# A hybrid attention and convolution layer on eight cores: casts ahead of the row factors, deferred VectorE work let out by a cost count, and the last output tile finished bank by bank

## What is computed

```python
h = rms_norm(x, norm_pre_w, NORM_EPS)
q, k, v, z_a, u_glu, z_c, ga, gc = split(h @ w_in)        # widths 1024 x4, 2048, 1024, 2048, 2048
q, k = partial_rotary(q), partial_rotary(k)               # 8 heads, two softmax maps of 64 each
o = diff_attention(q, k, v, lam)                          # softmax(q1 k1) v - lam softmax(q2 k2) v, causal
y_attn = (rms_norm(o, subln_w, SUBLN_EPS) * (1 - lam_init) * silu(z_a)) @ w_o_attn
u = causal_depthwise_conv(glu(u_glu + b_glu), w_dw, b_dw) # width 31
u = silu(layer_norm(u)) * silu(z_c)
y_conv = u @ w_pw2 + b_pw2
m = sigmoid(ga) * y_attn + sigmoid(gc) * y_conv
out = x + rms_norm(m @ w_out, norm_post_w, NORM_EPS)
```

## Time and profile before

| | us |
|---|---|
| median of 3 runs (lowest, highest) | 1183.71 (1183.11, 1189.87) |
| the profiled execution | 1181.25 |
| its span, slowest core | 1179.7 |
| TensorE busy | 1096.0 (93%) |
| VectorE busy | 551.1 (47%) |
| ScalarE busy | 323.7 (27%) |

### The profile page before, as it was taken

The page is one execution under the profiler, slowest core; times in us unless marked ns, Lnnn a source line. Parts: engine busy times, 40 slices in busy tenths (PEclk is TensorE's granted clock), DMA queues, the critical chain, the costliest instruction groups (busy, mean ns, idle before and its releaser), DMA issues.

```text
span 1179.7 us, 21808 instructions; the slowest of 8 cores (1168.9 to 1179.7 us)
## 1 busy us (share of the span) xinstructions
PE 1096.0 (93%) x8042; PEld 674.0 (57%) x8042; DVE 551.1 (47%) x1290; ACT 323.7 (27%) x500; POOL 102.1 (9%) x196
## 2 busy tenths in 40 slices
PE   2699999999999998899888999999999999999995
PEld 1355556886666774577444566666666666654442
DVE  5573444426556136766677633333333333315333
ACT  3442223432101165566444311111111111102111
POOL 1111010011101100000000001101101010000000
PEclk9899999999999998899899999999999999999998
DMA  8929767554665632322142305337266183064442
GB/s 251 220 46 174 143 114 150 106 86 81 139 135 113 139 57 57 57 49 51 37 73 37 55 18 108 55 53 114 46 128 110 34 144 57 16 179 161 158 160 95
DMA packets 49792, 118.11 MB, mean 100 GB/s; under 512 B 5520, under 2 KB 11920, under 8 KB 46352
## 3 DMA queue, kind: packets, MB, share of 16 engines
q0 software_dynamic: 27648, 62.93, 32.8%
q1 hardware_dynamic: 21744, 53.53, 14.9%
q10 hardware_dynamic: 288, 0.18, 0.0%
HBM read 162.94 MB, written 16.58 MB: 152 GB/s over the span
## 4 chain that ended last, share of the span: by engine, by line
PE 81%; DVE 9%; issue 3%; DMA 3%; ACT 3%; DVEq 0%; SPq 0%; ACTq 0%
PE ps L1291 21%; PE ps L816 11%; PE ps L1343 11%; PE ps L770 10%; PE ps L649 9%; PE ps L1301 5%; PE ps L1295 5%; PE ps L693 3%; PE ps L1021 2%; PE ps L922 2%; DMA r<-usc 2%; PE ps L899 2%; DVE zoz L970 1%; DVE r L1028 1%; DVE r L958 1%
## 5 line engine op out<-in xcount | busy, mean ns | idle before, releaser
L1291 PE MATMUL ps<-hTo,wring 128*128 128x384 bf16 x1536 | 257.5, 326 | 0.0
L1291 PEld LDWEIGHTS ps<-hTo,wring 128*128 128x128 bf16 x1536 | 150.3, 98 | 99.2
L164 POOL DMA_DIRECT2D wring<-wp x176 | 93.4, 549 | 835.9 <-PE ps L1291 242.0
L649 PE MATMUL ps<-hTo,wring 128*128 128x384 bf16 x768 | 130.9, 332 | 9.9 <-ACT hTo L545 4.2
L770 PE MATMUL ps<-wring,hTo 128*128 128x256 bf16 x1152 | 135.6, 273 | 1.2 <-PE ps L899 1.2
L1308 ACT ACTIVATE zoz<-zoz 128x384 f32<-128x384 f32 x96 | 50.0, 522 | 315.3 <-DVE zoz L1306 315.3
L816 PE MATMUL ps<-hTo,wring 128*128 128x384 bf16 x768 | 125.0, 326 | 0.0
L770 PEld LDWEIGHTS ps<-wring,hTo 128*128 128x128 bf16 x1152 | 108.6, 98 | 21.2 <-issue 8.3
L1306 DVE TENSOR_TENSOR zoz<-ps,R 128x384 f32<-128x384 f32 x96 | 53.5, 558 | 128.0 <-PE ps L1291 127.8
L649 PEld LDWEIGHTS ps<-hTo,wring 128*128 128x128 bf16 x768 | 75.6, 100 | 63.1 <-issue 16.5
L905 ACT ACTIVATE r<-ps 128x1024 bf16<-128x1024 f32 (+2 forms) x104 | 92.8, 905 | 47.6 <-PE ps L899 44.2
(11 more groups left out here) (114 smaller groups left out, 1016.1 us busy)
## 6 DMA issues: line engine op xcount, KB each, us to landing
wring<-wp POOLq DMA_DIRECT2D x176, 256.0 KB, 7.1
r<-usc SPq DMA_DIRECT2D x32, 295.2 KB, 8.2
hTo<-xr SPq DMA_DIRECT2D x9, 1024.0 KB, 6.8
out<-hTo SPq DMA_DIRECT2D x18, 512.0 KB, 3.3
r<-xf SPq DMA_DIRECT2D x11, 768.0 KB, 9.2
r<-wop POOLq DMA_DIRECT2D x4, 1024.0 KB, 13.8
zoz<-wop POOLq DMA_DIRECT2D x4, 1024.0 KB, 14.9
r<-wout POOLq DMA_DIRECT2D x4, 1024.0 KB, 20.5
```

Of the source, the lines that this page charges most:

```text
L164: eng.dma_start(out=it[1][0], in_=it[1][1]).then_inc(self.dsem[it[2]], 16)
L649: t.op('pe', lambda e, dc=dc, x=x: e.matmul(bank(2 * par + x, n), lhsT=w[:, dc, 128 * x:128 * x + 128], rhs=hTo[:, dc, c:c + n], start=(dc ...
L1291: t.op('pe', lambda e, dc=dc, k=k, w=w, o=o, cs=cs, c0=c0, n=n: e.matmul(o[k], lhsT=w[:, dc, cs], rhs=hTo[:, dc, HALO + c0:HALO + c0 + n], ...
```

## The change

1. **Start.** On the program's TensorE queue the first GLU stands ahead of the first column sums, quarter by quarter (`quart`). `own_run` is taken apart: the casts of the next group stand ahead of the roots and factors of the one before, squares and sums behind. `own_sums` loses its root and diagonals to a new `own_roots`. GLU pairs use banks 0/1, 2/3 or 4/5 by hand. The weight panel 3 waits for the last x quarter.
2. **Attention.** `run_late(H.rate)` gives way to `pump()`: two running sums, `now['pe']` and `now['dve']`, are raised by `spent` with costs written in the source; a deferred operation leaves the list only when `now['pe']` has reached its `ready` mark and `now['dve']` is at most 0.5 above it. `finalize` still forces what is older than four slots. The tanh and the two products of a z_conv evacuation go on a second list, `zlate`, from which one entry is taken at each step. The pieces are dealt out otherwise (`H.fill`): on the first half z_conv channel blocks 0 and 1 in the first pair of heads, 2 and 3 in the second, 4 in the third, 5 to 7 in the last, where it was 0, 1, 2 and 3 to 7.
3. **Merge.** The gates and y_conv of two blocks (`merge_head` 0 and 1) stand ahead of the last two heads' transposes.
4. **Last tile.** `g_last` squares each bank as it is finished and multiplies it; after the last bank come a reduction of four sums, the root, and four multiply-adds of 512 columns with a store each, by turns from the SP and ScalarE queues.

```diff
+            self.fill = ((('v', 1), ('z', 0, 1)), (('v', 2), ('z', 2, 3)), (('v', 3), ('z', 4)), (('z', 5, 6, 7),))
...
+        step = 4 if quart else 16
+        for k, (d0, x) in enumerate((d0, x) for d0 in range(0, 16, step) for x in (1, 0)):
+            for dc in range(d0, d0 + step):
...
+    def spent(e, us):
+
+        now[e] = (max(now['dve'], now['pe']) if e == 'dve' else now['pe']) + us
...
+        spent('pe', w / 1280.0)
...
+                spent('dve', 0.3)
...
+        spent('pe', 0.16 * len(todo))
...
+    def pump():
+
+        while late and late[0][1] <= now['pe'] and now['dve'] <= now['pe'] + 0.5:
+            run_late(1)
+
+    def run_zlate(flush=False):
+
+        while zlate:
+            zlate.pop(0)()
+            if not flush:
+                return
...
-        late.extend((fk, x) for x in f)
+        ready = now['pe'] + (2.0 if half == 0 else 0.0)
+        late.extend((fk, ready, 0.4, x) for x in f)
...
-            late.extend((fk + 1, x) for x in f)
+            late.extend((fk + 1, ready, 0.3, x) for x in f)
...
-            run_late(H.rate)
+            run_zlate()
+            pump()
...
+                run_zlate(True)
                 t.op('dve', lambda e: e.tensor_tensor(out=zv, in0=bank(b, n), in1=rv, op=ALU.mult), reads=[('ps', b)] + rn, writes=[('zt', p)])
...
+                zlate.extend((tanh, prods))
...
                 fill[done]()
+                spent('pe', 0.8)
+                pump()
...
+    glu_mm(0, 0, 0, quart=True)
     own_sums(0)
...
+    own_half(4)
+    own_half(5)
+    own_roots(0)
+    own_half(6)
+    own_half(7)
+    own_sq(4)
+    own_sq(5)
...
+    glu_mm(0, 1, 2, quart=True)
+    own_factors(0)
+    glu_ev(0, 0)
+    own_sum(4)
...
+    glu_mm(1, 2, 0)
     own_sums(2)
-    glu_mm(1, 2)
+    own_roots(2)
+    glu_mm(2, 2, 2)
     own_factors(2)
...
+                if it == 0:
+                    merge_head(0, 0, 0, 0)
+                    merge_head(1, 0, 0, 1)
+                    f_begin()
...
+        for k in range(4):
+            g_mm(i, k)
+            g_square(i, b0 + k, k)
...
+        g_root(i, [])
+        for k in range(4):
+            t.op('dve', lambda e, k=k: e.scalar_tensor_tensor(
+                out=ov(k), in0=ov(k), scalar=rstd2[:, i:i + 1], in1=xr[par][:, 512 * k:512 * k + 512], op0=ALU.mult, op1=ALU.add),
+                reads=[('xr', par), ('ol', k), ('rstd2', i)], writes=[('ol', k)])
+            t.dma(('sp', 'act')[k % 2], io["out"][i * 128:(i + 1) * 128, 512 * k:512 * k + 512], ov(k), reads=[('ol', k)], key=('outl', k))
```

More of the change, by code:

```diff
@@ L934, in run_late @@
         for _ in range(min(n, len(late))):
-            late.pop(0)[1]()
+            _, _, cost, f = late.pop(0)
+            spent('dve', cost)
+            f()
+    def pump():
[6 more added lines that the diff above has]
+                return
     def finalize(h, si, q0, nq):
@@ L1275, in f_begin, with merge_head @@
         wop_load(1)
-    it = 0
-    for pi in range(8):
+    def merge_head(it, pi, ci, tg):
         sa, sc = (2 * pi) % 4, (2 * pi + 1) % 4
@@ new lines, in merge_head @@
+        cs = slice(128 * ci, 128 * ci + 128)
+        c0, n = H.fg[tg]
+        b0 = 4 * (it % 2)
+        for k, w, slot in ((0, wga, sa), (1, wgc, sc)):
+            for dc in range(16):
+                t.op('pe', lambda e, dc=dc, k=k, w=w: e.matmul(
+                    bank(b0 + k, n), lhsT=w[:, dc, cs], rhs=hTo[:, dc, HALO + c0:HALO + c0 + n], start=(dc == 0), stop=(dc == 15)),
+                    reads=[('W', slot, dc // 4)] + own_res, writes=[('ps', b0 + k)], sig=(dc == 15))
+        for fc in range(8):
+            t.op('pe', lambda e, fc=fc: e.matmul(
+                bank(b0 + 3, n), lhsT=wopb[pi % 2][:, 1, fc, cs], rhs=uT[:, fc, 32 + c0:32 + c0 + n], start=(fc == 0), stop=(fc == 7)),
+                reads=[('wop', pi % 2)] + [('u2T', c, tg) for c in range(8)], writes=[('ps', b0 + 3)], sig=(fc == 7))
@@ new lines, in merge_tail @@
+    def merge_tail(it, pi, ci, tg):
+        nch = pi * 2 + ci
+        cs = slice(128 * ci, 128 * ci + 128)
+        c0, n = H.fg[tg]
+        b0 = 4 * (it % 2)
+        for fc in range(8):
+            t.op('pe', lambda e, fc=fc: e.matmul(
+                bank(b0 + 2, n), lhsT=wopb[pi % 2][:, 0, fc, cs], rhs=ozT[:, fc, c0:c0 + n], start=(fc == 0), stop=(fc == 7)),
+                reads=[('wop', pi % 2)] + ozT_all, writes=[('ps', b0 + 2)], sig=(fc == 7))
+        Rg = R1[:, HALO + c0:HALO + c0 + n]
+        f1v, f2v, sgav, sgcv = (v[:, 0:n] for v in (f1, f2, sga, sgc))
+        for k, sg, nm in ((0, sgav, 'sga'), (1, sgcv, 'sgc')):
+            t.op('dve', lambda e, k=k, sg=sg: e.tensor_tensor(out=sg, in0=bank(b0 + k, n), in1=Rg, op=ALU.mult), reads=[('ps', b0 + k)] + own_r, writes=[nm])
+            t.op('act', lambda e, sg=sg: e.activation(out=sg, in_=sg, func=AF.Sigmoid), reads=[nm], writes=[nm])
+        t.op('dve', lambda e: e.tensor_tensor(out=f1v, in0=bank(b0 + 2, n), in1=sgav, op=ALU.mult), reads=[('ps', b0 + 2), 'sga'], writes=['f1'])
+        t.op('dve', lambda e: e.scalar_tensor_tensor(out=f2v, in0=bank(b0 + 3, n), scalar=bpw2x[:, nch:nch + 1], in1=sgcv, op0=ALU.add, op1=ALU.mult),
+             reads=[('ps', b0 + 3), 'sgc', 'bpw2x'], writes=['f2'])
+        t.op('dve', lambda e: e.scalar_tensor_tensor(out=mT[:, nch, c0:c0 + n], in0=f2v, scalar=0.5, in1=f1v, op0=ALU.mult, op1=ALU.add),
+             reads=['f1', 'f2'], writes=[('mT', nch, tg)])
@@ L1318, in program @@
+    it = 0
+    for pi in range(8):
+        for ci in range(2):
+            for tg in range(NG):
+                if it == 0:
+                    merge_head(0, 0, 0, 0)
+                    merge_head(1, 0, 0, 1)
+                    f_begin()
+                elif it > 1:
+                    merge_head(it, pi, ci, tg)
+                merge_tail(it, pi, ci, tg)
+                it += 1
         for n in (2 * pi + 4, 2 * pi + 5):
@@ L1356, in g_out @@
              reads=pres + ['small'], writes=['junkG', ('ssq2', i)])
[L1357 to L1359 removed]
+        g_root(i, pres)
         for hh in range(2):
@@ L1379, in program @@
     g_out(1)
-    for i in range(2, NT):
+    for i in range(2, NT - 1):
         for npn in range(4):
             g_mm(i, npn)
-        if i + 1 < NT:
-            g_load(i + 1)
+        g_load(i + 1)
         g_out(i)
-    t.wait_all_dma('sp', [('out', p, hh) for p in range(2) for hh in range(2)])
+    g_last(NT - 1)
+    t.wait_all_dma('sp', [('out', p, hh) for p in range(2) for hh in range(2)] + [('outl', k) for k in range(4)])
 def host_consts(inputs, H):
```

196 lines of the change are left out of this document (96 added, 100 removed).

## The result

| | before | after |
|---|---|---|
| median, us | 1183.56 | 1214.35 |
| lowest to highest (4 runs each) | 1183.11 to 1189.87 | 1213.62 to 1215.65 |
| ratio, 95% interval | | 1.025, 1.022 to 1.028 |

The account below looks back on a forecast made before the run. TensorE and VectorE taken as level in the attention, so VectorE's queue order decides; first half -2 - 36.9 + 32.5 + 3 + 15 + 12 - 3 = +20.6, giving median 1204 us; range 1190 to 1216, over all 1160 to 1214.

Parts of the forecast that it names:

- the strings ahead of the copy: Ends of heads 3 to 7: 19 to 29 forced deferred operations delay ScalarE's slot copy; stalls in heads 3 to 6, +32.5.
- the range over all: Whole kernel's time, all cases together: from the second half's 1160 to 1214 us.
- start: Up to the first convolution: casts ahead of roots and factors gain 2 us, from -5 to +1.
- attention, what goes: First half's attention: exponentials no longer queue behind late evacuations; 22.3 us of waits and 14.6 of low clock go, -36.9.
- what comes, in the heads: First half's attention: forced operations stall TensorE, +32.5 in heads 3 to 6, +3 in head 1, +15 for clock.
- what comes, at the end: End of attention into merge: 29 forced and 48 left operations delay the first tail, +8.3, and +3.7 for clock: +12.
- last tile: After TensorE's last matmul: 7.9 us of ScalarE and VectorE become 4.9 to 5.2, -3, bounds -2 and -4.
- The second half: Odd cores: nothing forced, accumulator copy waits of 6.1 us and perhaps 2 of others go; 1171.2 - 12 = 1159.
- The faster one: Attention: strings run before their slots end, first half near 1138, second sets 1163; chance 0.28 together with the third rival.
- the even one: Attention: strings cost half (31 of 62 us), all 36.9 won: 1173, with less won up to 1185; chance 0.22.
- The third: Only the attention's end stalls (+12), second half sets 1163; chance 0.28 together with the strings-run-early rival.
- the marks set for it: Signs in heads 3 to 6, attention clock, merge transposes and first convolution that would show the forecast (chance 0.5) right.

Follow-up runs that it names:

- x6: Changed kernel with margin 4.0 on the first half alone and z_attn's banks begun at 2, 3 in place of 0, 1; 1157.55 us, ratio 0.975.
- x9: Changed kernel with both costs of a deferred operation at 0.28 us in place of 0.4 and 0.3; 1192.67 us, ratio 1.008.
- x3: Changed kernel, but a slot's end forces what is older than three slots, not four; 1184.68 us, ratio 1.002.
- x7: x6 with tanh and products of a z_conv evacuation put back right behind its first multiplication; 1175.48 us, ratio 0.993.
- x10: x6 with the pieces dealt as before the change, on both halves; 1156.31 us, ratio 0.978.
- x11: x6 with a margin of 2.0 on the first half, where it was 4.0; 1159.52 us, ratio 0.978.
- x5: Changed kernel with margin 4.0 on the first half alone and the start of before; 1161.30 us, ratio 0.979.
- x1: Changed kernel with the pacing alone undone: six (second half four) deferred operations at each step; 1177.23 us, ratio 0.996.
- x4: Changed kernel with the start of before: casts behind the factors, banks by turns; 1211.94 us, ratio 1.025.
- x8: Kernel before with the last tile's new ending alone; 1181.59 us, ratio 0.998.

## Why the prediction came out as it did

The direction held, and so did the main mechanism, the strings ahead of the copy. 1204 was forecast, slower, and 1214.35 came: inside the forecast's own range (1190 to 1216), a third of a microsecond above the range over all (1160 to 1214), whose upper end had been set below the forecast's own. The terms of the sum for the first half, core 6. What goes and what comes can be told apart by x6, which has the changed attention without the strings; its first y_attn matmul starts 236.1 us after its first QK (413.5 to 649.6), before it was 258.2 (415.4 to 673.6), after it is 294.4 (419.5 to 713.9).

| term | forecast | measured | from |
|---|---|---|---|
| start | -2 | +4.1 | first QK 415.4, 419.5 |
| attention, what goes | -36.9 | -28.6 | 236.1 - 258.2, less the 6.5 of merge done earlier |
| what comes, in the heads | +50.5 | +46.4 | 264.1 - 217.7, after and x6 |
| what comes, at the end | +12 | +13.7 | 30.3 - 18.4 from the last QK to the first y_attn, and 1.8 behind it |
| last tile | -3 | -2.5 | 13.7, 11.2 |
| sum | +20.6 | +33.1 | spans: 1212.8 - 1179.7 = 33.1 |

(50.5 is 32.5 + 3 + 15. The 1.8 is what the stretch from the first y_attn to the last matmul grew beyond the 6.5: 487.7 against 492.4 - 6.5 = 485.9 us, with y_attn's first matmuls at the low clock.)

**The strings** were right one by one, each within 0.6 us. Forecast 8.4, 6.1, 11.1 and 6.9 us for heads 3 to 6, measured 7.80, 6.04, 10.52 and 7.17; these four make 31.5 of the 46.4. The walk along VectorE's queue, priced from start to start and not by busy time, carried it, with what else stands in the queues counted at each place; x9 confirms it with other lengths: four stalls each within 0.35 us of what was expected. x3 confirms that the copy is what passes the string on to TensorE.

**The start** is the first step that failed, by 6.1 us. It treated the GLU banks as of no account. The hand-set bases shift the turn of banks, so the last GLU pair ends in 0 and 1, which z_attn takes first; before, it ended in 2 and 3. TensorE waits 4.24 us there, on the other half 4.38. With the 2.7 us that the matmuls behind it lose by the lower clock this is what failed. Nor is the -2 itself shown. With the banks turned round (x6) the first QK comes 1.9 us earlier than before on core 6, but core 6 was the latest of its half before, and such starts differ by some microseconds from core to core and run to run (in x11 411.1 to 418.2). Averaged over the four cores of the first half it is 414.4 before, 418.8 after, and 413.6 to 414.6 in the four runs with mended banks (x6, x7, x10, x11); the spans of x5 and x6 give 0.7 us. Little of the reading time won reached even the first convolution: it came at 109.4 instead of 111.08 (on average over the half 1.2 us earlier), for the three GLUs ahead of it took 18.32 us instead of 15.76, at a granted clock of 0.85 between 91 and 109 us where it was 1.00.

**What goes** was 8.3 us too large. It took all 22.3 us of idleness and all of the low clock. x6 keeps 16.4 us idle of 235 (31.8 before), so 15.4 went, and its clock of 0.99 over that stretch still costs about 2 us of the 14.6. "At best" stood in the text beside the number, and the sum used it all the same. The term was also put down to one part of the change, the split, and the pacing was counted as a cost only. x1 and x7 show that the split without the pacing, or the pacing without the split, shortens the attention by 3 or 4 us only, the new deal included, and that deal, which got no term, is worth 4.6 beside the other two (x10). This number came nearer than its reason.

These two terms together were 14.4 us too low, the one for the heads 4.1 too high, and the second hid a part of the first; that is luck.

**The last tile**: the steps are as priced, 0.60 for the square (forecast 0.6), 0.69 for the product (0.7), 2.74 for the four (0.7 each). The last store was issued at about 1206.3, 4.7 us after the last matmul's end where it was 8.0 before. With 2.9 us (median of the two on ScalarE's queue) some 7.6 us lie between the last matmul and its landing, just within 7.5 to 8.5. The engines gained 3.3 us, and from the last issue to the span's end it took 6.5 us where it was 5.7, so 2.5 are left. The last stores of 256 KB took 2.3 us on SP's queue (two) where those of 512 KB took 2.6 (three). The Trainium skill, DMA: Bandwidth & Descriptors, section Anatomy of one DMA, gives its fixed part and rate for DMAs issued by GpSimd; the 0.6 us that was estimated from it for the halved size was 0.3 on SP's queue, and on the path that ends last, 2.9 us on the other queue, there was no gain at all.

**The second half** was put at 1159 and came at 1161.8 on core 5. Its wait for the copy went from 6.1 to 1.9 us, where the forecast had taken all of it off; the start took 4.38 back by the banks, and the start of before (x4) would have made it 6.6 us shorter.

**The rivals.** The faster one (strings run before slots end) fell: no string started early. Of the even one, "half of the strings' cost", x3 shows what it would have taken: the buffer freed one slot earlier, 1184.68. The third, only the end stalls, was part of the truth (9.1 and 3.0 us there) beside the heads.

Of the marks set for it: ScalarE's copy waited 7.83, 7.17, 10.33 and 11.19 us for L994 in heads 3 to 6 (6 or more); TensorE waited 36.9 for L981 in all and 31.5 of it in heads 3 to 6 (25 or more); the clock was 0.88 in the attention's second stretch (below 0.9; over the whole attention it was 0.92); 9.1 at the transposes (8 or more); the first convolution at 109.4 (106 to 112). That last mark was too weak: it was met, and the start still lost 4 us further on.

What stays open: no run takes the merge's new order out alone, or tries another margin than 0.5 or 4.0 on the second half, and which of TensorE's waits cost it clock and which do not is not settled.

## What to carry to other kernels

A rule that holds deferred work back until a sum allows it must be read together with the place that forces it out: where the two engines are level, a margin of 0.5 us against 4.0 decided over 59 us on the half that sets the time, and each operation more in a string added its start-to-start time, about 0.27 us, to the stall. If a buffer must be forced free, do it a slot before its next writer needs it. When instructions are re-ordered by hand, follow the rotation of banks to the next stage too, since a turn by one pair cost a wait of 4.2 us, and 2.7 us of lower clock behind it, where nothing had been changed.

## What the runs showed of the hardware that was not expected

A stall of TensorE can cost twice, by itself and by the clock behind it. The second stretches of the attention: 0.88 with three waits of 6 to 10.5 us in it and a fourth just ahead (after), 0.92 with none over 4.5 us (before), 0.93 with none over 2.5 us in it and one of 2.8 just ahead (x7), 0.98 with none over 1.8 us (x6). Length is not all of it: x7's first stretch has waits of 1.9, 1.9 and 2.1 us and that of 2.8 at its end, and its clock is 0.99.

Among the last stores of the kernel, halving the size from 512 to 256 KB took 0.3 us off 2.6 on SP's queue, while the same 256 KB issued from ScalarE's queue took 2.9 (two or three stores each; 2.4 and 2.8 in x6, 2.4 and 3.0 in x8).
